# A weight slot's 512-column and 256-column products: alternating, or the eight of one width ahead of the eight of the other

## The reference, cut to what matters

```python
z = h @ w_in                                   # 2048 x 7176: attention and a recurrence
y = concat([y_fox, o_b]) @ w_out               # 2048 x 2048
u = h @ w_up ; f = (silu(gate) * up) @ w_down  # 2048 x 11264, 5632 x 2048
gate = sigmoid(rms_norm(h) @ w_ple_gate)       # 2048 x 2048
q, k, v = split(h @ w_qkv, 3) ; x = x + o @ w_o
x = x + relu(rms_norm(x) @ w1) ** 2 @ w2       # 2048 x 8192, 8192 x 2048
```

## Time and profile before

| | |
|---|---|
| runs | 2425.62 us median of 3 (2425.12 to 2425.65) |
| profiled execution, its own time | 2425.61 us |
| its span, first to last instruction | 2423.8 us |
| PE busy | 2411.3 us (99%) |
| PEld, DVE, ACT busy | 2051.3, 1526.7, 1216.3 us |
| the chain that ended last | 96% PE, 2% DVE |
| PE's granted clock | full in all 40 slices |

### The profile page before, as it was taken

One profiled execution on the slowest core, in us unless ns is written; L12 is line 12 of the kernel. 1 busy time (PEld: TensorE's weight loads), 2 busy tenths in 40 slices (PEclk: granted clock), 3 DMA queues, 4 the chain that ended last, 5 costly groups with the idle time before them and its releaser, 6 DMA issues.

```text
span 2423.8 us, 30523 instructions
## 1 busy us (share of the span) xinstructions
PE 2411.3 (99%) x12352; PEld 2051.3 (85%) x12352; DVE 1526.7 (63%) x1788; ACT 1216.3 (50%) x1596; POOL 110.0 (5%) x122
## 2 busy tenths in 40 slices
PE   8999999999999999999999999999999999999999
PEld 7898888788888888888877888888888888888887
DVE  6676765577567657667666666665665555554554
ACT  6455444565445445445565655555443443443442
POOL 0221310000000000000000211000000000000000
PEclk9999999999999999999999999999999999999999
DMA  9566566556655655655655565455566566556664
GB/s 307 141 173 174 155 197 192 179 174 196 199 186 175 207 175 189 201 175 189 214 188 166 182 192 167 148 180 183 183 191 192 181 195 196 184 189 194 189 198 150
DMA packets 327132, 451.27 MB, mean 186 GB/s; under 512 B 14528, under 2 KB 209344, under 8 KB 326352
## 3 DMA queue, kind: packets, MB, share of 16 engines
q1 hardware_dynamic: 324592, 440.52, 58.0%
q0 software_dynamic: 2256, 8.80, 1.2%
q10 hardware_dynamic: 144, 0.01, 0.0%
HBM read 447.17 MB, written 2.10 MB: 185 GB/s over the span
## 4 chain that ended last, share of the span: by engine, by line
PE 96%; DVE 2%; issue 0%; ACT 0%; DMA 0%; POOL 0%; SPq 0%; DVEq 0%; ACTq 0%
PE main L566 92%; PE aux L566 3%; DVE LO L1152 1%; DVE AR L1152 1%; PE aux L579 1%; ACT HI L810 0%; PE aux L677 0%; PE aux L695 0%; DMA RAW<-in_w_in 0%; DVE AR L1329 0%; DVE AR L1155 0%; DVE XT L1155 0%; PE aux L661 0%; DVE AR L1293 0%; DVE AR L1294 0%
## 5 line engine op out<-in xcount | busy, mean ns | idle before, releaser
L1152 DVE TENSOR_TENSOR LO<-RAW,HI 128x1024 fp32r<-128x1024 f32 (+2 forms) x833 | 1009.2, 1232 | 617.8 <-ACT HI L810 616.5
L810 ACT ACTIVATE HI<-RAW 128x1024 fp32r<-128x1024 f32 (+2 forms) x833 | 850.1, 1045 | 624.5 <-PE main L566 578.6
L566 PE MATMUL main<-XT,HI 128*128 128x512 f32 x2944 | 1037.7, 397 | 0.0
L566 PE MATMUL main<-XT,LO 128*128 128x256 f32 x2944 | 825.6, 280 | 0.0
L566 PE MATMUL main<-HI,YT 128*128 128x512 f32 x2240 | 693.5, 390 | 0.0
L566 PEld LDWEIGHTS main<-XT,HI 128*128 128x128 f32 x2944 | 552.5, 188 | 131.9
L566 PEld LDWEIGHTS main<-XT,LO 128*128 128x128 f32 x2944 | 556.1, 189 | 0.4
L566 PEld LDWEIGHTS main<-HI,YT 128*128 128x128 f32 x2240 | 420.4, 188 | 87.6
L566 PE MATMUL main<-HI,XT 128*128 128x512 f32 (+1 forms) x1472 | 457.9, 386 | 8.6 <-DVE LO L1152 8.5
L566 PE MATMUL main<-LO,YT 128*128 128x512 f32 x1120 | 435.8, 389 | 0.0
L566 PEld LDWEIGHTS main<-HI,XT 128*128 128x128 f32 x1472 | 274.6, 188 | 61.2 <-DVE XT L1155 7.1
(11 more groups left out here) (87 smaller groups left out, 669.5 us busy)
## 6 DMA issues: line engine op xcount, KB each, us to landing
RAW<-in_mlp_w SPq DMA_DIRECT2D x256, 512.0 KB, 4.2
RAW<-in_w_up SPq DMA_DIRECT2D x176, 512.0 KB, 4.8
RAW<-in_na_w_qkv SPq DMA_DIRECT2D x96, 512.0 KB, 4.3
RAW<-in_w_in SPq DMA_DIRECT2D x95, 512.0 KB, 4.4
RAW<-in_w_down SPq DMA_DIRECT2D x88, 512.0 KB, 4.7
RAW<-in_w_out SPq DMA_DIRECT2D x32, 512.0 KB, 4.4
RAW<-in_w_ple_gate SPq DMA_DIRECT2D x32, 512.0 KB, 4.5
RAW<-in_na_w_o SPq DMA_DIRECT2D x32, 512.0 KB, 4.2
```

The lines of the kernel that those rows point to most:

```text
L566: return L.e.matmul(out, l, r, start=start, stop=stop, skip_group_check=True)
L810: return L.e.activation(out, x, f, **kw)
L1152: return L.e.tensor_tensor(out, x, y, op)
```

## The change

In a w slot the four chunks are walked through twice. The first walk issues the eight 512-column products of the high weights, the second the eight 256-column products of the low weights. The wait for the high part (`a_hi`) stands at the head of the slot, that for the low part (`v_lo`) between the walks. The products themselves, their operands, their accumulators and the order of q and m within a walk are the same; so is everything outside `w_slot`.

```diff
             def w_slot(b, j, cs, out, first, last):
                 hi, lo = parts(HI, j, 256), parts(LO, j, 256)
                 A = XT if b.src == "x" else YT
+                L.wait_ge(S("a_hi"), j + 1)
                 for q, c in enumerate(cs):
                     L.wait_ge(S(inputs(b, c)[0]), inputs(b, c)[1])
-                    if q == 0:
-                        L.wait_ge(S("v_lo"), j + 1)
-                    final = q == len(cs) - 1
                     for m in range(2):
-                        ns = slice(m * 128, m * 128 + 128)
-                        mm(out[:, m, :], hi[:, q, ns], A[:, c, :, :].rearrange("p a t -> p (a t)"), first and q == 0, False)
-                        x = mm(out[:, m, 256:512], lo[:, q, ns], A[:, c, 0, :], False, last and final)
+                        mm(out[:, m, :], hi[:, q, m * 128:m * 128 + 128], A[:, c, :, :].rearrange("p a t -> p (a t)"), first and q == 0, False)
+                L.wait_ge(S("v_lo"), j + 1)
+                for q, c in enumerate(cs):
+                    for m in range(2):
+                        x = mm(out[:, m, 256:512], lo[:, q, m * 128:m * 128 + 128], A[:, c, 0, :], False, last and q == len(cs) - 1)
                 x.then_inc(S("p_use"), 1)
```

## The result

The changed kernel takes 2419.24 us, the median of ten runs (2418.96 to 2419.51), beside 2425.54 us for the kernel before: a ratio of 0.9974, 95% interval 0.9966 to 0.9982. It is 6.3 us faster, where 11.8 us were forecast (2413.8 us). The profiled execution's span is 2417.2 us.

What follows compares the result with a forecast made beforehand. PE, busy 99% at full clock, was taken as the bound. Pairs at 226.7 + 120.7 = 347.4 ns gained 10.6 us, lost 0.3 and gained 1.5, together 11.8: 2425.6 - 11.8 = 2413.8 us, range 2405 to 2432.

Steps and rivals of the forecast that it cites:

- likeliest case: 256-column products in w slots cost 118 to 122.5 ns each, giving 2406 to 2419 us; chance 0.48.
- three signs that it named for being wrong: 256-column products 0.127 us apart, 512-column products not keeping 0.227 us, or w stretches keeping two kinds.
- The bound and the waits: PE, 99% busy at full clock, sets the time; each w slot's second wait costs nothing, at most some 1 us.
- The narrow products: Eight 256-column products in a row in each w slot were taken at 120.7 ns each.
- the 344-column run: Eleven short fp32r products in a 344-column block, 157.3 ns each, 14.0 ns beyond their columns; gave the 120.7 ns.
- the row of the first pair: Start of a w stretch: 256-column product succeeded after 0.11 us, the 512-column product behind it took 0.24 us.
- The wide products: Eight 512-column products in a row in each w slot were taken at 226.7 ns each, as in x stretches.
- The 350 ns taken for the short stretches: Price of each of 560 pairs in short w stretches between small products; 1.5 us gained at 347.4 ns.
- Rival 1: Load and hand-over in series make 256-column products 126.7 ns: 2431.3 us; chance 0.24 with what lies beyond.
- Rival 2: Each product keeps its cost whatever its neighbours, both kinds of w stretch stay: 2425.6 us; chance 0.18 with nearby outcomes.
- Rival 3: 256-column products hold 113.3 ns through a walk, 21.8 us less than forecast: 2392.0 us; chance 0.10.
- the dear kind: Six long w stretches at 353.3 ns a pair (one product of each width), 6.4 ns above the other two.

Runs made afterwards that it cites:

- the runs of sixteen: Against the changed kernel, every second slot of a block issues its 256-column products first and its 512-column ones last; 2415.83 us, ratio 0.9959.

## Why the prediction was right, and by how much it was off

The time fell, as forecast, and the long w stretches came to be of one kind. The size was off: 6.3 us instead of 11.8, just above half. The measured 2419.24 us lies at the far edge of what the prediction called its likeliest case (2406 to 2419), and the stated range of 2405 to 2432 us held a time without any gain as well, so that lying in it says little. One of the three signs that it named for being wrong came true: the wide products didn't keep 0.227 us.

**The bound and the waits: right.** PE at full clock is the bound before and after, the x stretches are unchanged, and the waits are worth nothing, shown by the two runs that took order and waits apart.

**The narrow products: right.** The prediction took 120.7 ns from the 344-column run. In sixteen they cost 120.0, in eight 119, since the first has its successor's start after 113 ns, just as the row of the first pair showed.

**The wide products: the term that was mis-sized.** The prediction took 226.7 ns from the x stretches and from the first product of a w stretch, both behind wide products. Behind narrow ones they cost 230.0. The pair comes to 349.1 instead of 347.4 ns, and 1.7 ns x 2,944 = 5.0 us, which takes 2413.8 to 2418.8, within 0.5 us of the measured 2419.2. The sign of it stood in the earlier trace rows: the 512-column product behind the first narrow one took 0.24 us. I read that as the repayment of a start recorded early. In the changed kernel the repayment is larger than the gain: the wide run of an inner slot is 0.03 us longer than that of the entry slot (some 27 ns by the single starts), for 8 ns gained in the narrow one. The 350 ns taken for the short stretches was a guess at the middle; with their edges they cost 353.0 before and 352.7 after and gave 0.2 us, where 1.5 were forecast.

**The rivals.** Rival 1 (load and hand-over in series, 126.7 ns) is refuted: a floor of 111 ns there is, but the 13.3 ns don't come behind it, since the 256-column products come every 120 ns and not every 126.7. Rival 2 (order doesn't matter) is refuted by the change and by the runs of sixteen, though its remark that something else chooses between the two kinds was true: the beginning of the stretch does. Rival 3 (113 ns sustained) holds for the first narrow product of a run and then no more.

**The reason I gave for the dear kind.** I laid the dear kind's 6.4 ns to the alternation. That was wrong in one half: alternation has no cost of its own, as the better kind, and 2413.8 us with a cut, show. It was the state in which an alternating stretch had settled.

What stays open is the mechanism inside TensorE by which 20 ns build up and are paid. The runs show its size by run length, that 20 ns are paid even where the loads have 35 ns of room, and that it depends on what went before. They don't show which queue or unit holds it, nor whether the narrow or the wide run's length sets the smaller payments.

## What to carry to other kernels

When PE is busy for 99%, look at the cost of a product from start to start, stretch by stretch. The same instructions can run at two steady rates, here 346.7 and 353.3 ns a pair, and which one may hang on a single product at the beginning. Try more than one length of run: two and sixteen beat eight here, and four gained almost nothing. Or find the beginning that puts an alternating stretch into its cheap state. Price a product next to the neighbours that it will have, behind as well as ahead of it: here the forecast used the right narrow price and the wrong wide one.

## What the runs showed of the hardware that I had not expected

- An alternation of 512- and 256-column fp32r products, each with its load, has two steady rates, 346.7 and 353.3 ns a pair. Each holds for over a hundred us, and one narrow product cut into 128+128 columns moves a stretch from the dear one to the cheap one, in four of six tries inside a stretch and at all eight beginnings where it was tried (seven in one kernel, one in another).
- Passing from narrow to wide products costs nothing in the cheap state of the alternation, 6.7 ns in the dear one, 3.3, 17, 20 and 20 ns where both widths go in runs of 2, 4, 8 and 16. In runs of eight it is also 20 ns when the narrow ones have 320 columns, and about 40 ns when they have 128.
- In runs of one width, fp32r products with a load each cost their columns at 2.4 GHz and about 13.3 ns: 120.0 ns for 256 columns, 146 for 320, 226.7 for 512. With 128 columns, each with a load of 128, they come 111 ns apart, where columns and 13.3 ns would be 67.
